# Four edits to a two-block transformer kernel: who copies the turned keys, how the first weights arrive, how the last query job ends

## The reference, cut to what matters

```python
qkv = silu(causal_depthwise_conv((x @ w_in)[:, :3072], conv_w))      # first product of the kernel
q, k, v = split(qkv, 3); q = l2_normalize(q) * 128**-0.5; k = l2_normalize(k)

# gated delta rule, per chunk of tokens and per head (8 heads of 128)
decay = where(causal, exp(g_cum[t] - g_cum[s]), 0)
a_mat = where(strict, (beta * k) @ k.T * decay, 0) + I               # solved against the values and the keys
qk    = (q @ k.T) * decay
v_new = u - w @ state;  out = (q * exp(g_cum)) @ state + qk @ v_new;  state = state * exp(g_last) + k_dec.T @ v_new

# MLA queries: 16 heads of 96, RMS norm per head, rotation of the last 32 of each
q = rope(rmsnorm((cq @ w_uq).reshape(S, 16, 96), q_norm))
```

## Time and profile before

| | |
|---|---|
| median of 3 runs | 2141.86 us (2138.47 to 2143.8) |
| the profiled execution | 2138.05 us, its span 2135.8 us |
| mean granted clock of TensorE | 0.983 |
| PE busy | 2048.0 us (96% of the span) |
| DVE busy | 995.8 us (47%) |
| ACT busy | 464.4 us (22%) |
| POOL busy | 270.2 us (13%) |

### The profile page before, as it was taken

How to read it: one execution, slowest core, us unless ns; L and a number is a source line. 1 busy time by engine, 2 the same in 40 slices (tenths; PEclk the granted TensorE clock), 3 DMA queues, 4 the chain that set the end, 5 groups by cost and what they waited for, 6 DMA issues and landing times. The chain is left out here.

```text
span 2135.8 us, 20381 instructions
## 1 busy us (share of the span) xinstructions
PE 2048.0 (96%) x7558; PEld 1138.2 (53%) x7558; DVE 995.8 (47%) x1776; ACT 464.4 (22%) x1006; POOL 270.2 (13%) x348
## 2 busy tenths in 40 slices
PE   8999999999999999999899999999998999999995
PEld 4444444578874445444445468554445568644442
DVE  2445544567673124333544656253344467433333
ACT  1111111022341001100331146220004446420000
POOL 1000000011011000433100000003321000003333
PEclk9999999999999999999999999999999999999998
DMA  5223365510022124799536920138993220045996
GB/s 180 90 97 128 123 250 201 185 51 1 1 79 94 60 85 157 277 408 393 222 130 206 323 109 2 47 137 339 403 388 119 84 79 2 3 157 195 375 373 250
DMA packets 122468, 363.29 MB, mean 170 GB/s; under 512 B 27580, under 2 KB 30936, under 8 KB 109824
## 3 DMA queue, kind: packets, MB, share of 16 engines
q1 hardware_dynamic: 76816, 174.13, 23.0%
q10 hardware_dynamic: 30432, 157.30, 18.8%
q0 software_dynamic: 15120, 30.53, 4.1%
HBM read 335.60 MB, written 43.52 MB: 178 GB/s over the span
## 5 line engine op out<-in xcount | busy, mean ns | idle before, releaser
L1605 PE MATMUL bank<-ring,work 128*128 128x512 f32 x768 | 344.3, 602 | 3.3 <-DVE work L1621 3.3
L1605 PEld LDWEIGHTS bank<-ring,work 128*128 128x128 f32 x768 | 144.5, 193 | 169.1 <-issue 169.1
L1904 POOL DMA_INDIRECT work<-x_rows,small x168 | 169.2, 1007 | 271.4 <-DVE work L1869 203.0
L1616 PE MATMUL bank<-ring_halves,work 128*128 128x512 f32 x384 | 172.8, 593 | 4.0 <-DVE work L1630 4.0
L423 PE MATMUL bank<-featT,ring 128*128 128x512 f32 x384 | 170.4, 597 | 3.8 <-DMA ring<-in_w_in 3.8
L1333 PE MATMUL bank<-ring,work 128*128 128x512 f32 x384 | 168.1, 597 | 2.9 <-PEq L2169 1.9
L2394 PE MATMUL bank<-ring,featT 128*128 128x512 f32 x384 | 168.8, 601 | 1.6 <-DVE small L2483 1.6
L1627 DVE TENSOR_TENSOR work<-work,bank 128x256 f32<-128x256 f32 x48 | 20.2, 421 | 284.1 <-ACT work L1624 284.1
L2394 PEld LDWEIGHTS bank<-ring,featT 128*128 128x128 f32 x384 | 73.7, 193 | 93.7 <-issue 91.9
L1616 PEld LDWEIGHTS bank<-ring_halves,work 128*128 128x128 f32 x384 | 72.7, 190 | 95.1 <-issue 95.1
L1333 PEld LDWEIGHTS bank<-ring,work 128*128 128x128 f32 x384 | 72.9, 192 | 92.0 <-issue 92.0
(11 more groups left out here) (443 smaller groups left out, 2780.8 us busy)
## 6 DMA issues: line engine op xcount, KB each, us to landing
ring<-in_w_in SPq DMA_DIRECT2D x16, 2048.0 KB, 11.8
ring<-in_moe_w_gate ACTq DMA_DIRECT2D x28, 1024.0 KB, 6.4
ring<-in_moe_w_up ACTq DMA_DIRECT2D x28, 1024.0 KB, 8.8
ring_halves<-in_moe_w_down ACTq DMA_DIRECT2D x28, 1024.0 KB, 9.6
ring_halves<-in_w_ada SPq DMA_DIRECT2D x48, 512.0 KB, 6.9
y_rows<-work ACTq DMA_DIRECT2D x48, 512.0 KB, 9.9
ring<-in_expert_w_gate ACTq DMA_DIRECT2D x14, 1024.0 KB, 7.9
ring<-in_expert_w_up ACTq DMA_DIRECT2D x14, 1024.0 KB, 11.1
```

Of the source, the lines that this page charges most:

```text
L1605: last = nc.tensor.matmul(gu_sum[par], xgT[par][:, k, :], w_gu[par][:, k, :, :], start=(k == 0), stop=(k == KD - 1))
L1616: last = nc.tensor.matmul(bank[5 + h][:, :], hT[par][:, k, :], w_dn[par][:, k, span(h)], start=(k == 0), stop=(k == KF - 1))
L1904: nc.gpsimd.indirect_dma_start(out=xg[par][:, s * QD:(s + 1) * QD], out_offset=None, in_=x_quarters, in_offset=bass.IndirectOffsetOnAxis(a ...
```

## The change

1. Delta rule, keys: the two copies of the turned keys go from VectorE, where they stood after "clip", to ScalarE, between "rest" and "decay". TensorE waits for ScalarE's copies; ahead of the unit whose product goes to bank 0 it also waits for VectorE's first difference, which reads that bank.
2. Delta rule, `qk`: VectorE's two products with the decay go from before level 1 to before level 6.
3. Chunk 0 of `w_in` is loaded by two DMAs of 256 columns each (1 KB of each row), each with a semaphore of its own; TensorE waits for the first ahead of block 0, for the second ahead of block 2.
4. The last query job of MLA is handed over by halves: ScalarE squares and then copies half 0 when its three products are done, then half 1; VectorE sums the squares by halves, scales and adds epsilon, and waits for the second copy before it rotates.

```diff
-    def plan(self, parts, slot=None, by_loop=False):
+    def plan(self, parts, slot=None, by_loop=False, own=None):
...
-        self.count[slot] += 16 * len(parts)
+        if own is None:
+            self.count[slot] += 16 * len(parts)
+        self.own.append(own)
...
-            for dst, src in self.chunks[self.issued]:
-                sp.dma_start(dst(self.slot(self.issued)), src).then_inc(self.landed[self.slots[self.issued]], 16)
+            own = self.own[self.issued]
+            for i, (dst, src) in enumerate(self.chunks[self.issued]):
+                sp.dma_start(dst(self.slot(self.issued)), src).then_inc(own[i] if own else self.landed[self.slots[self.issued]], 16)
...
-        plan_cols(w_in, 0, 3 * DN)
+        first_landed = [sem(f"first_landed{i}") for i in range(2)]
+        W.plan([(lambda s, i=i: s[:, 0:KD * BANK].rearrange("p (k n) -> p k n", k=KD)[:, :, 2 * P * i:2 * P * (i + 1)],
+                 rows(w_in)[:, :, 2 * P * i:2 * P * (i + 1)]) for i in range(2)], own=first_landed)
+        plan_cols(w_in, BANK, 3 * DN)
...
-                    if b % 4 == 0:
+                    if b in (0, 2):
+                        pe.wait_ge(first_landed[b // 2], 16)
+                    if b >= 4 and b % 4 == 0:
                         W.wait_landed(pe, chunk)
...
-                    DV.wait(pe, ("kT", 1), c)
+                    AC.wait(pe, ("kT", 1), c)
                     for u in units:
+                        if UNIT_BANK[u] == 0:
+                            DV.wait(pe, ("diff", 0), c)
...
                     AC.done(nc.scalar.activation(e_rest, e_rest, ACT.Exp), "rest")
+                    PE.wait(act, "kT", c)
+                    for h in halves:
+                        AC.done(nc.scalar.activation(kT[:, hs(h), :], b4(5 + h), ACT.Copy), ("kT", h))
...
-                    PE.wait(dve, "kT", c)
-                    for h in halves:
-                        DV.done(nc.vector.tensor_copy(kT[:, hs(h), :], b4(5 + h)), ("kT", h))
...
-                    for h in halves:
-                        PE.wait(dve, ("qk", h), c)
-                        DV.done(nc.vector.tensor_tensor(qk[:, hs(h), :], b4(5 + h), decT[:, hs(h), :], ALU.mult), ("qk", h))
                     for l in LV:
+                        for h in halves if l == NL - 1 else ():
+                            PE.wait(dve, ("qk", h), c)
+                            DV.done(nc.vector.tensor_tensor(qk[:, hs(h), :], b4(5 + h), decT[:, hs(h), :], ALU.mult), ("qk", h))
...
-                    PE.done(last, ("q", j))
+                        if j == len(q_jobs) - 1:
+                            PE.done(last, ("q_half", h))
+                    if j < len(q_jobs) - 1:
+                        PE.done(last, ("q", j))
...
+                j, (p, t) = len(q_jobs) - 1, q_jobs[-1]
+                for h in range(2):
+                    src = bank[2 * (j % 4) + h][:, 0:half]
+                    PE.wait(act, ("q_half", h))
+                    DV.wait(act, ("q_ssq", j - 2))
+                    AC.done(A(squares[j % 2][:, h * half:(h + 1) * half], src, ACT.Square), ("half_square", h))
+                    AC.done(A(q_m[:, t, (2 * p + h) * half:(2 * p + h + 1) * half], src, ACT.Copy), ("half_copy", h))
...
+                        n = PAIR // 2
+                        for h in range(2):
+                            AC.wait(dve, ("half_square", h))
+                            DV.done(V.reduce_sum(q_root[:, lo + n * h:lo + n * (h + 1)],
+                                                 squares[j % 2][:, n * QK * h:n * QK * (h + 1)].rearrange("p (h n) -> p h n", h=n), X_AXIS), ("half_ssq", h))
+                        DV.wait(dve, ("half_ssq", 1))
...
+                    if j == len(q_jobs) - 1:
+                        AC.wait(dve, ("half_copy", 1))
```

More of the change, by code:

```diff
@@ L72, in __init__ @@
         self.turn = 1
-    def plan(self, parts, slot=None, by_loop=False):
+        self.own = []
+    def plan(self, parts, slot=None, by_loop=False, own=None):
         if slot is None:
@@ L784, in build @@
                 [(s, h) for s in ("ks", "qs") for h in halves] + [("vn", h) for h in halves] + ["z"] + [(s, h) for s in ("o", "s") for h in halves])
-        ac_n = ([("qT", 0), ("qT", 1), "g", "e", "rest", "decay"] +
+        ac_n = ([("qT", 0), ("qT", 1), "g", "e", "rest", ("kT", 0), ("kT", 1), "decay"] +
                 [(s, l, h) for l in LV for s in ("lev",) + (("turn",) if l == L_WIDE else ()) for h in units] + [("vn", h) for h in halves] + ["z"])
-        dv_n = (["g_key", "rest", ("diff", 0), ("diff", 1), "clip", ("kT", 0), ("kT", 1)] + [(s, u) for u in units for s in ("neg", "first", "t0")] +
-                [("qk", h) for h in halves] + [(s, l, h) for l in LV for h in units for s in ("add",) + (("turn",) if l < L_WIDE else ())] +
+        dv_n = (["g_key", "rest", ("diff", 0), ("diff", 1), "clip"] + [(s, u) for u in units for s in ("neg", "first", "t0")] +
+                [(s, l, h) for l in range(1, NL - 1) for h in units for s in ("add",) + (("turn",) if l < L_WIDE else ())] +
+                [("qk", h) for h in halves] + [("add", NL - 1, h) for h in units] +
                 [(s, h) for h in halves for s in ("rk", "r")] + [(s, h) for s in ("oq", "sg", "o", "s") for h in halves])
@@ L2588, in build @@
         pe_n += [("lat", 0, 3), ("turned_lat", 0, 2), ("lat", 1, 2), ("turned_lat", 0, 3), ("lat", 1, 3), ("turned_lat", 1, 2), ("turned_lat", 1, 3)]
-        pe_n += [("kv", j) for j in range(len(kv_jobs))] + [("q", j) for j in range(len(q_jobs))]
+        pe_n += [("kv", j) for j in range(len(kv_jobs))] + [("q", j) for j in range(len(q_jobs) - 1)] + [("q_half", h) for h in range(2)]
         ac_n = cb_b.row_names() + cb_b.norm_names(0) + cb_b.keep_names(0, 0) + cb_b.norm_names(1) + cb_b.norm_names(2) + lat_names[0](0) + cb_b.keep_names(1, 0)
@@ L2595, in build @@
             ac_n += [("k_log", t), ("k_root", t)] if n == NKV - 1 else []
-        for j in range(len(q_jobs)):
+        for j in range(len(q_jobs) - 1):
             ac_n += [("q_copy", j), ("q_square", j)]
+        ac_n += [("half_square", 0), ("half_copy", 0), ("half_square", 1), ("half_copy", 1)]
         ac_n += ["q_log", "q_exp"]
@@ L2608, in build @@
         for j in range(len(q_jobs)):
-            dv_n += [("q_ssq", j)] + (["q_mean", "q_eps2"] if j == len(q_jobs) - 1 else []) + [("rope", j, i) for i in range(6)]
+            dv_n += ([("q_ssq", j)] if j < len(q_jobs) - 1 else [("half_ssq", 0), ("half_ssq", 1), "q_mean", "q_eps2"]) + [("rope", j, i) for i in range(6)]
             dv_n += unit_names(T - 1) if j == 0 else []
@@ L2705, in _ @@
                                                     start=(k == 0), stop=(k == KQ - 1))
-                    PE.done(last, ("q", j))
+                        if j == len(q_jobs) - 1:
+                            PE.done(last, ("q_half", h))
+                    if j < len(q_jobs) - 1:
+                        PE.done(last, ("q", j))
                     if t == T - 1:
-                        W.mark_used(uq_ids[p], PE.sem, PE.value(("q", j)))
+                        W.mark_used(uq_ids[p], PE.sem, PE.value(("q", j) if j < len(q_jobs) - 1 else ("q_half", 1)))
             @block.scalar
@@ L2769, in _ @@
                         AC.done(A(r, r, ACT.Exp, scale=-0.5), ("k_root", t))
-                for j, (p, t) in enumerate(q_jobs):
+                for j, (p, t) in enumerate(q_jobs[:-1]):
                     half = PAIR * QK // 2
@@ L2878, in _ @@
                     lo = t * NHB + p * PAIR
[L2879 to L2882, removed]
+                    if j < len(q_jobs) - 1:
+                        AC.wait(dve, ("q_square", j))
+                        DV.done(V.reduce_sum(q_root[:, lo:lo + PAIR], squares[j % 2].rearrange("p (h n) -> p h n", h=PAIR), X_AXIS), ("q_ssq", j))
+                    else:
+                        n = PAIR // 2
[4 more added lines that the diff above has]
+                        DV.wait(dve, ("half_ssq", 1))
                         DV.done(V.tensor_tensor(T4(q_root, NHB), T4(q_root, NHB), per_t(q_inv2), ALU.mult), "q_mean")
```

## The result

The changed kernel takes 2129.53 us (median of 8 runs, 2124.74 to 2134.43), the kernel before 2139.69 us (8 runs beside them, 2137.23 to 2143.8). The ratio is 0.9949 [0.9939, 0.9959]: faster by 0.51%, or 10.9 us; the medians differ by 10.2. 12.3 us were forecast. That the median stands 0.1 us from the forecast one is luck: the forecast was made from 2141.86, the kernel before was 2.2 us faster in the runs beside the changed one, and one of the four edits missed its gain. The profiled execution took 2128.86 us, with a span of 2126.8 (before: 2138.05 and 2135.8).

A forecast was written before the change was run, and what follows sets the result against it. TensorE, busy 2048.0 of 2135.8 us, was taken as the bound, so only its idle or low-clock time pays. 2.55 + 3.96 + 2.5 + 1.7 + 1.6 = 12.3 us off the median 2141.86 gave 2129.6, range 2124 to 2137.

The forecast's parts named there:

- The spare 0.2 us: Delta rule: cover of 0.2 us in each of its two edits before the next operand would hold the work.
- rival (b): Delta rule: waits only replaced, the next operand 0.5 us late, 3.5 of 6.5 us given back; 2133.1 us, chance 0.11.
- Rival (d): Delta rule keys: ScalarE's copies come later than VectorE's did, so moving them gives 0; 2132.2 us, chance 0.03.
- The clock gain above it (up to 1.7): Attention stage's start: a gap of 3.3 for 4.9 us may shorten the low clock by one stretch, upper gain 3.3.
- So w_in's slow stretches are slow in bytes: First weights' load: limited by bytes, not rows, so the half part lands at 13.8 instead of 16.31, gaining 2.5 us.
- rival (a): First weights: half chunk limited by rows, lands when the whole did, clock drops; gain 8.1, 2133.8 us, chance 0.16.
- The clock's term: Behind the first weights' gap: with about 1.3 us of gap TensorE keeps full clock; gain 1.7, between 0 and 1.7.
- Rival (c): First weights: chunk 1's issue held behind two 1024-row DMAs, SP and TensorE late; 2147.5 us, chance 0.03.

The follow-up runs named there:

- fill_gap: Changed kernel plus three thrown-away products in TensorE's wait for the first weights; ratio 0.9954 [0.994, 0.9969] against the kernel before.
- query_only: Kernel before with only the last query job of MLA handed over by halves; ratio 0.9987 [0.9977, 0.9998], median 2136.63 us.
- the other matrix: Changed kernel with chunk 0's two column parts read from `w_dn_out` instead of `w_in`; one execution, profile only, second stage starts at 196.87.
- weights_only: Kernel before with only chunk 0 of `w_in` loaded in two column parts; ratio 0.9997 [0.9988, 1.0006], median 2137.32 us.
- row_halves: Changed kernel with chunk 0 cut into 512 full rows per part, blocks 0 to 3 multiplied in two groups; ratio 0.9921 [0.9906, 0.9935], median 2124.24 us.
- row_halves_fill: `row_halves` plus three thrown-away products on TensorE ahead of the attention stage's transposes; ratio 0.9920 [0.9908, 0.9933], median 2122.17 us.
- no_weights: Changed kernel with chunk 0 of the weights in one DMA again; ratio 0.9959 [0.9944, 0.9974], median 2131.40 us.

## Why the prediction was right or wrong

**Edit 1** (forecast 2.55): right in place, mechanism and size; 2.8 measured. **Edit 2** (3.96): right; 4.4 measured. Both were slightly too small. The spare 0.2 us on which they rested was there, so rival (b), that the waits are only replaced, fell: no wait of L837, L853 or L857 for another engine came in. Rival (d) fell with them, as the copies on ScalarE end 2.1 us ahead of k k^T.

**Edit 4** (1.6): right; 1.55 in every kernel that has it. The clock gain above it (up to 1.7), kept only for the range, isn't settled. The loss at the attention stage's start fell from 2.67 to 1.42 us in these two executions, but it lies between 1.4 and 2.9 in the others. Of the seven profiled executions with a gap of 3.4 us three have one low stretch of 3.4 us behind it (`fill_gap` and `query_only` besides the changed kernel) and four have 6.8 us; all six with a gap of 4.9 us have 6.8.

**Edit 3** (2.5 and 1.7 for the clock): wrong. The first step that failed is the sentence "So w_in's slow stretches are slow in bytes". It was concluded from 64-byte rows of `w_in` at 380 packets per us and from 1152-byte rows of another matrix. Neither was a 1 KB row of `w_in` in the first microseconds of its load, and there the chunk goes at about 100 rows a microsecond for either row size.

A second step stands in no sentence: that the first part is complete once that much has been moved. The later rows were faster than the rate that the forecast took, so that 1024 rows were begun 5.5 us after 8.0, where it had 5.8 us for all. (Its working was a little short there: 0.35 against 0.41 MB per us is 15 to 17%, not 12%.) But the part's last count came 2.2 us later, at 15.72, when over half of the second part's rows had been begun; the forecast had nothing for that. So the outcome is that of rival (a), which had a chance of 0.16, but its reason, a limit by rows, explains only a part of it. Measured starts with column parts are 15.77, 16.03 and 16.51 us, against 16.13 to 17.03 with the whole chunk: about 0.5 us, not 2.5.

The clock's term hung on this: a gap of "about 1.3" was to keep the clock up, but the gap stayed at 3.06. Where gaps of 3.1 to 4.4 us stayed at this place, the low clock came behind eight of nine, and where the row cut, the other matrix or useless products had closed the gap to 0.8 us it came in none of five. The gap of 3.30 us (`weights_only`) had no low clock behind it, 3.78 (before) had one stretch, and 3.06 (after) two. The Trainium skill's page "TensorE: Matmul & The Clock Gate", section "HAM oscillation — how this bites in real kernels", says that such a gap can bring the clock down for the work behind it, and the runs agree.

**Rival (c)**, the slower side, didn't come: SP was through at 9.48 us and took up the conv stage on time. Its condition (chunk 1's issue held behind two DMAs of 1024 rows) wasn't met. In the conv stage SP was held longer than before: its first two issues took 2.78 and 9.36 us, against 0.37 and 6.43. Nothing waited for those loads, so this cost nothing.

**The sum.** 12.3 was forecast. By the measured pieces it is 7.15 + 1.55 + 0.5 = 9.2, less 1.2 for the clock at the start in the profiled execution: 8.0, near rival (a)'s 8.1. The medians say 10.2, the ratio 10.9 (8.8 to 13.1). Between the two spans 9.0 us were gained, 1.0 more than the 8.0. That is the net of many steps both ways, the largest of them where the low clock differs: 1.7 gained between 860 and 1030 us and 1.4 between 1934 and 2108 us, where only the kernel before has the low clock, or has it for longer, and 1.7 lost at each of 1113 and 1346 us, where the changed kernel has more of it. The rest between 8.0 and 10.2 or 10.9 isn't assigned. So the total fell near the forecast with a wrong step inside it: the total alone would not have shown that, `weights_only` did.

## What to carry to other kernels

If a load must be halved so that work can begin sooner, look first whether it goes by rows: compare packets per microsecond, not MB, for two row sizes of the same matrix in the same stretch. If it goes by rows, cut it by rows and let the products be summed in two groups, as `row_halves` does. Look also at when the last count of the first part's semaphore arrives, and not only at how much has been moved: a second part in the same queue can be under way while the first lacks its last rows. On a kernel whose TensorE is 96% busy, price each wait from start to start along the order of the work, and look whether the engine that takes over has a gap there; the two moves of the delta rule came out within 0.5 us of that.

## What the runs showed of the hardware

**Rows of `w_in`.** From 9 to 11 us rows of 1 KB go at 101 and 119 a microsecond, and from 11 to 15 us at 235 to 295. The whole chunk's rows of 2 KB go at 97 in each of the first two microseconds, then at 146 to 202 up to 16 us; those of `row_halves` at 105, then at 168 to 198 up to 15 us. The slow rate isn't only one of the start: in chunk 1 of the kernel before, 85 to 105 rows of 2 KB are begun in each microsecond from 18 to 23 us. Why the rate changes, and what in the 32,832 bytes between them does it, stays open: only the matrix was exchanged, which changes the distance and the place in memory together. The Trainium skill's page "DMA: Bandwidth & Descriptors", section "Latency and other measured facts", gives lower rates for rows that lie large powers of two apart, 164 GB/s at 2 MiB and 103 at 4 MiB against a full 214. No run here shows that; the distance here is far smaller and no power of two.

**The clock between equal executions.** Adding up, over all stretches of 1 us, TensorE's busy share times what the granted clock lacks of full gives 25.2 us for the kernel before, 26.8 for the changed one, 26.4 for its repetition, and 18.0 (`row_halves_fill`) to 32.0 (`no_weights`) over the fourteen profiled executions. This is a measure of low clock and not of time lost from end to end: the changed kernel has 1.7 us of it at 1028 to 1032 us that the kernel before lacks, but its next wait (L2037 in the kernel before) is shorter, 4.23 against 5.85 us, and from L2012's first product to L2037's both take 19.9 to 20.0 us. Not every stretch has a gap ahead of it. In all fourteen executions the clock falls while TensorE is busy with 64 products of only 16 columns each (L2372 in the kernel before, from 1120.01 us; 1111.19 in the changed one), 2.7 to 5.0 us behind the first of them, and it stays low for 6.8 to 13.7 us. Elsewhere some stretches come in some executions only, also between two executions of the same kernel. That is a spread of several microseconds by itself, as large as the whole of edit 4 or the low clock at the start. For `fill_gap` the profile shows such a stretch taking back the gain; for `row_halves_fill` the record shows only that the gain is smaller than the intervals can tell.
